# Moving the second token half's gating branch of a mixer behind the first row fetches, and the first fetched rows into attention buffers

## The reference, cut to what matters

```python
def mix_branches(q, k_all, v_all, z, gate_logits, ...):
    o = diff_attention(q, k_all, v_all, lam)
    o = rmsnorm(o, subln_g) * (1.0 - lam_init)
    y_attn = o.reshape(B, L, ATTN_OUT) @ w_branch_attn
    y_sgu = spatial_gating(gelu(z), sgu_ln_g, sgu_ln_b, sgu_w, sgu_b) @ w_branch_sgu
    g_attn, g_sgu = jnp.split(jax.nn.sigmoid(gate_logits), 2, axis=-1)
    return (g_attn * y_attn + g_sgu * y_sgu) @ w_out

def spatial_gating(z, ln_g, ln_b, w_s, b_s):
    u, v = jnp.split(z, 2, axis=-1)
    v = layernorm(v, ln_g, ln_b)
    ...
    mixed = jnp.einsum('gpq,bnqgc->bnpgc', w_s, vb) + ...
    return u * mixed.reshape(B, L, SGU_W)

def peer(h, w_query, sub_keys, u_tab, v_tab):
    q = rmsnorm((xt @ w_query).reshape(T, PEER_HEADS, 2, PEER_PK_DIM))
    s = jnp.einsum('thpd,pnd->thpn', q, sub_keys)
    # two top-16 lists a head, their 256 sums, top 16 of them: eidx, gate
    ...
    act = gelu(jnp.einsum('td,thkd->thk', xb, u_tab[ib])) * gb
    return jnp.einsum('thk,thkd->td', act, v_tab[ib])
```

## Time and profile before

| | before |
|---|---|
| median of 3 runs | 2083.95 us (2083.92 to 2088.63) |
| the profiled execution | 2088.11 us |
| its span | 2086.3 us |
| busy PE / DVE / ACT / POOL | 71% / 37% / 21% / 15% of the span |
| read from HBM | 796.98 MB, 383 GB/s on average |
| first row fetch | at 1402.00 us of the span |

### The profile page before, as it was taken

The page is one execution under the profiler, slowest core; times in us unless marked ns, Lnnn a source line. Parts: engine busy times, 40 slices in busy tenths (PEclk is TensorE's granted clock), DMA queues, the critical chain, the costliest instruction groups (busy, mean ns, idle before and its releaser), DMA issues.

```text
span 2086.3 us, 27127 instructions
## 1 busy us (share of the span) xinstructions
PE 1476.3 (71%) x11468; PEld 647.3 (31%) x11468; DVE 782.1 (37%) x1941; ACT 430.1 (21%) x1013; POOL 304.8 (15%) x290
## 2 busy tenths in 40 slices
PE   9999566877565555689899999986767744444444
PEld 7654122422111112234334445563235410000001
DVE  5832010000000000000122265547767677867764
ACT  1331100000000000011000145643245622221212
POOL 0010000000000000000000000004344444544441
PEclk9999788888878887799999999997788855555556
DMA  9798999999999999999998754469999999999997
GB/s 406 287 404 369 388 428 428 426 429 427 428 427 429 427 428 426 423 406 419 404 414 347 296 187 146 164 261 390 415 422 420 420 420 421 421 421 420 421 421 304
DMA packets 78057, 800.00 MB, mean 383 GB/s; under 512 B 9232, under 2 KB 9360, under 8 KB 10736
## 3 DMA queue, kind: packets, MB, share of 16 engines
q1 hardware_dynamic: 40304, 529.61, 60.9%
q0 software_dynamic: 37632, 268.65, 31.1%
HBM read 796.98 MB, written 1.05 MB: 383 GB/s over the span
## 4 chain that ended last, share of the span: by engine, by line
PE 42%; DMA 41%; DVE 9%; ACT 3%; issue 2%; POOL 2%; SPq 0%; DVEq 0%; ACTq 0%; POOLq 0%
DMA AR<-in_peer_uv,AR 14%; DMA AR<-in_w_gate 10%; DMA AR<-in_w_up 10%; PE PS L811 6%; PE PS L745 6%; DMA AR<-in_w_down 5%; PE PS L443 4%; PE PS L776 4%; DVE AR L1695 3%; PE PS L454 3%; PE PS L891 2%; POOL AR L2128 2%; PE PS L1027 2%; PE PS L984 2%; PE PS L707 1%
## 5 line engine op out<-in xcount | busy, mean ns | idle before, releaser
L745 PE MATMUL PS<-AR 128*32 128x512 f32 x2048 | 316.0, 751 | 200.4 <-DMA AR<-in_w_up 110.8
L1027 PE MATMUL PS<-AR 32*32 32x512 f32 x4032 | 225.5, 931 | 289.8 <-ACT AR L2063 289.7
L2128 POOL DMA_INDIRECT AR<-in_peer_uv,AR x256 | 288.8, 1128 | 967.4 <-DVE AR L1686 665.3
L1695 DVE CUSTOM_DVE_ANT_0 AR<-AR 128x1024 f32<-128x1024 f32 x256 | 309.3, 1222 | 161.7 <-DMA AR<-in_peer_uv,AR 161.3
L1323 DVE TENSOR_TENSOR AR<-AR,PS 128x512 f32<-128x512 f32 x16 | 11.0, 688 | 571.9 <-PE PS L745 571.9
L745 PEld LDWEIGHTS PS<-AR 128*32 128x32 f32 x2048 | 63.6, 124 | 422.7 <-DMA AR<-in_w_up 173.2
L776 PE MATMUL PS<-AR 128*32 128x256 f32 x2048 | 148.1, 439 | 53.5 <-DMA AR<-in_w_down 53.5
L1027 PEld LDWEIGHTS PS<-AR 32*32 32x32 f32 x4032 | 37.4, 125 | 432.6 <-ACT AR L2063 426.9
L811 PE MATMUL PS<-AR 128*128 128x512 f32 x336 | 154.2, 602 | 0.0
L776 PEld LDWEIGHTS PS<-AR 128*32 128x32 f32 x2048 | 68.8, 123 | 139.4 <-DMA AR<-in_w_down 70.0
L443 PE MATMUL PS<-AR 128*128 128x512 f32 x224 | 102.1, 610 | 1.9 <-DVE AR L1093 1.9
(11 more groups left out here) (320 smaller groups left out, 1592.3 us busy)
## 6 DMA issues: line engine op xcount, KB each, us to landing
AR<-in_w_up SPq DMA_DIRECT2D x64, 2048.0 KB, 17.4
AR<-in_w_down SPq DMA_DIRECT2D x64, 2048.0 KB, 14.5
AR<-in_w_gate SPq DMA_DIRECT2D x63, 2048.0 KB, 20.9
AR<-in_w_in SPq DMA_DIRECT2D x33, 1024.0 KB, 7.4
AR<-in_w_ada SPq DMA_DIRECT2D x12, 2048.0 KB, 13.2
AR<-in_w_out SPq DMA_DIRECT2D x6, 2048.0 KB, 8.9
AR<-in_w_in SPq DMA_DIRECT2D x5, 2048.0 KB, 14.0
AR<-in_peer_w_query SPq DMA_DIRECT2D x5, 2048.0 KB, 11.5
```

The lines of the kernel that those rows point to most:

```text
L745: x = pe.matmul(PS[32 * q:32 * q + 32, bk, :], XS[e][:, j, :], src[:, q * 512:(q + 1) * 512], start=(j == 0), stop=(j == 7), skip_group_ch ...
L1027: x = pe.matmul(PS[c:c + 32, ACC[a][g], :], DI[t, p, r, :], AR[t, off + 1024 + m * 512:off + 1536 + m * 512], start=(h == 0 and p == 0), s ...
L1695: v.tensor_tensor_reduce(rows, rows, HB[:, a, :], 1.0, 0.0, MULT, ADD, DOT[:, ix, k:k + 1]).then_inc(*w.hit("dot", ix, k))
L2128: pool.indirect_dma_start(out=AR[:, off:off + 2048], out_offset=None, in_=D["peer_uv_2"], in_offset=bass.IndirectOffsetOnAxis(ap=EI[:, ix, ...
```

## The change

Four things change together.

1. In the list of stages, `rest.z2.1 rest.z0.1 bend.z2.1 bend.z0.1 zn1.1 zn2.1 zn3.1` leave the attention part and stand between `rt5.0 qse.1.0` and `row.0.0`. `zmix.1`, `zturn.1 bend.gs.1 bs.0.1`, `bs.1.1` and `bend.ga.1` go into the row loop, at rows 2, 4, 6 and 7. From `ba.1.1` on, what `late` inserts comes 6 rows later.
2. The first five rows go to attention buffers, which are free after `av 15`; rows 5 and 6 go to the slot of the first `wq`. Two of the five are given up after row 11 (they become the buffer of w_op for half 1), one before the second half's queries.
3. SP loads z2 and z0 of half 1 into the halves of one slot, at `take.0`. w_bs 1 of half 1 takes that slot after z0 has been used. w_ba 0, w_ba 1 and w_op 0 of half 1 no longer go out at `av 15`: w_ba 0 waits for `bs.0.1`, w_ba 1 for `ba.0.1`, w_op 0 for `v.0.5` (rows 10 and 11), and so on.
4. Two small buffers move (`G2`, `SG2`), with the waits that belong to them.

```diff
-                    "rest.gs.0 bend.ga.0 bend.gs.0", "rope.q.0.1 rope.q.1.1 bs.0.0", "bs.1.0", "rest.z2.1", "rest.z0.1"]
+                    "rest.gs.0 bend.ga.0 bend.gs.0", "rope.q.0.1 rope.q.1.1 bs.0.0", "bs.1.0", "", ""]
...
-            do("bend.z2.1 bend.z0.1")
-            steps(pairs[3], [("ba", 1, 0), ("bae", 1, 0), ("zn1", 1)], pairs[4], [("yt", 0), ("yte", 0), ("zn2", 1), ("zn3", 1)])
-            steps(pairs[5], [("op", 0, 0), ("ope", 0, 0)], pairs[6], [("op", 1, 0), ("ope", 1, 0), ("zmix", 1)], pairs[7])
+            steps(pairs[3], [("ba", 1, 0), ("bae", 1, 0)], pairs[4], [("yt", 0), ("yte", 0)])
+            steps(pairs[5], [("op", 0, 0), ("ope", 0, 0)], pairs[6], [("op", 1, 0), ("ope", 1, 0)], pairs[7])
             do("rest.gs.1")
-            steps([("up1", 0), ("up2", 0)], [("zturn", 1)], pairs[8], [("fn1", 0), ("fn2", 0)], pairs[9], [("ft", 0), ("fte", 0)], pairs[10])
+            steps([("up1", 0), ("up2", 0)], pairs[8], [("fn1", 0), ("fn2", 0)], pairs[9], [("ft", 0), ("fte", 0)], pairs[10])
...
-            do("bend.gs.1 bend.ga.1 bs.0.1 bs.1.1")
+            do("rest.z2.1 rest.z0.1 bend.z2.1 bend.z0.1 zn1.1 zn2.1 zn3.1")
...
-            late = {12: [("hn1", 1)], 14: [("hn2", 1), ("ht", 1)], 18: [("hte", 1)], 22: [("ba", 0, 1)], 25: [("bae", 0, 1)],
-                    26: [("ba", 1, 1)], 29: [("bae", 1, 1)], 30: [("yt", 1)], ...
+            late = {2: [("zmix", 1)], 4: [("zturn", 1), ("bend", "gs", 1), ("bs", 0, 1)], 6: [("bs", 1, 1)], 7: [("bend", "ga", 1)], 12: [("hn1", 1)], ...
+                    32: [("ba", 1, 1)], 35: [("bae", 1, 1)], 36: [("yt", 1)], ...
...
-        RING = [3, 4, 5, 2]
+        RING = [5, 2, 3, 4]
...
-            for i, event in ((2, ("wq", 0, 0)), (0, ("w_bs", 0, 1)), (1, ("w_bs", 1, 1))):
-                free.update({k: ("used", *event) for k in halves[i]})
+            free.update({k: ("mm", "av", 15) for k in (W0 + 2048, o + 2048, o, o + 16384, o + 18432)})
+            free.update({k: ("used", "wq", 0, 0) for k in halves[2]})
...
                 elif stage == "take" and x[0] == 0:
-                    for n in range(2):
-                        square(("w_bs", n, 1), "w_branch_sgu_2", n)
-                    assert turn[0] % 4 == 2
+                    assert turn[0] % 4 == 0
+                    user[S50] = user[S51] = user[5]
+                    for slot, m in ((S50, "z2"), (S51, "z0")):
+                        load(slot, ("w_in2", m, 1), D["w_in_2"][PAIRS.index(m), 3].rearrange("p (n j c) -> p n j c", n=2, j=2), 2, 2, 512)
+                    user[5] = user[S51]
+                    turn[0] += 1
+                    square(("w_bs", 0, 1), "w_branch_sgu_2", 0)
                     for n in range(2):
                         square(("wq", n, 0), "peer_w_query_2", n)
-                    w.wait_ge("mm", "av", 15)
-                    for slot, key, name, n in ((NS, "w_ba", "w_branch_attn_2", 0), (NS + 4, "w_ba", "w_branch_attn_2", 1),
-                                               (NS + 5, "w_op", "w_out_2", 0)):
+                    square(("w_bs", 1, 1), "w_branch_sgu_2", 1)
+                    for slot, key, name, n in ((RING[1], "w_ba", "w_branch_attn_2", 0), (NS + 5, "w_op", "w_out_2", 0),
+                                               (RING[1], "w_ba", "w_branch_attn_2", 1)):
+                        if key == "w_op":
+                            for k in (o + 16384, o + 18432):
+                                w.wait_ge(*GIVEN[k])
                         load(slot, (key, n, 1), weight(name, n), 8, 512)
```

29 lines of the change are left out of this document (17 added, 12 removed), and 6 rows, old and new, of the table late.

## The result

The changed kernel takes 2135.85 us (median of 4 runs, 2132.22 to 2137.52) where the kernel before takes 2083.93 beside it: a ratio of 1.024 [1.022, 1.026], 52 us more. The forecast was 29 us more. The direction was right, the size was not, and the time lies outside the range.

The account below looks back on a forecast made before the run. The row loop was taken as bound by bytes at 421 GB/s. An earlier first row (-11.7), more bytes behind it (+20.0) and more lost time (+20.8) made +29 us on 2084: 2113 us, range 2095 to 2129.

Parts of the forecast that it names:

- Term 1: Attention chain: steps taken off it let the first row fetch start 11.7 us earlier, bounds 8 to 15.
- T0: Start of row 0, the first row fetch: 1402.00 us before the change, forecast at 1390.3.
- Term 2: Row loop: four more weight loads, 8.4 MB, move behind the first row fetch and cost 20.0 us at 421 GB/s.
- Term 3: First rows up to v.0.3: ends at T0 + 66, DMA engines stand 23.7 us against 2.9, +20.8 us.
- Later losses I leave as they are: Row loop behind v.0.3: time lost there, 4.3 us between 1435 and 1510, was taken as unchanged.
- The rival of a second starvation: Row loop at op.1.1: PE waits for the late w_op 1 load; if uncovered, 10 us more, 2123; 5 in 100.
- The fed loop: First rows: DMA engines stay fed, so term 3 is 0 or -2.9 us, time 2089 to 2092; 12 in 100.
- the faster one: Attention shrinks by 20 us and DMA engines lose nothing: -7 us, 2077; 7 in 100.
- the start that does not move: Another attention wait replaces the filler, first fetch stays at 1402: +41 us, 2125; 6 in 100.
- The late loads: Sign in the profile: four weight loads more behind the first row fetch, about 287 MB from there to the end.
- the idle times of DVE before L1516: Sign in the profile: DVE idles twice before reading bs, released by PE, 5 us and more each.

Follow-up runs that it names:

- b_order: Kernel before, with zn1.1 moved behind yte.0 and rest.gs.1 moved into a place where PE waits: 2081.1 us, ratio 0.9981.
- a_drop_one: Changed kernel without the load of w_ba 1 of half 1, its products reading w_ba 0, no wait added: 2128.98 us, ratio 1.0213.
- b_late_loads: Kernel before, with w_ba 0, w_ba 1 and w_op 0 of half 1 waiting for the row loop's second v instead of av 15: 2094.58 us, ratio 1.006.
- a_drop_early: Changed kernel without the loads of w_bs 1 and w_ba 0, their products reading w_bs 0: 2132.59 us, ratio 1.0244.
- a_spread: Changed kernel with op.1.1 at row 50 instead of 44 and what follows up to 4 rows later: 2130.84 us, ratio 1.0224.
- a_swap: Changed kernel with the loads of wq 3 and wq 0 exchanged between their two slots: 2130.33 us, ratio 1.0212.
- a_eight_late: Changed kernel with one more row buffer, the eighth, from row 36 on: 2129.2 us, ratio 1.021.
- a_swap_spread: Changed kernel with wq 3 and wq 0 exchanged between their slots and op.1.1 at row 50: 2125.44 us, ratio 1.0205.
- a_best2: Changed kernel with DVE reading bs behind rows 7 and 10, wq 3 and wq 0 exchanged, op.1.1 at row 50, extra row buffer from the start: 2109.77 us, ratio 1.0115.
- a_best: Changed kernel with z chain behind the first rows, wq 3 and wq 0 exchanged, op.1.1 at row 50, extra row buffer from the start: 2116.48 us, ratio 1.0166.
- a_z_loop: Changed kernel with the z chain behind the first rows and both bs steps two rows later: 2130.99 us, ratio 1.0226.

## Why the size was wrong, point by point

- **Term 1, T0 earlier.** Forecast 11.7, measured 11.3 as T0 - M. One trace is good to some 3 us here: the fifteen kernels with the changed attention have 195.7 to 200.9, mean 197.9, and the three with that of before 209.3 to 210.9, mean 210.0, which makes 12.1. So the sum holds. Its parts were not measured one by one, and that it came out within 0.4 us is in part luck. b_order has 6.3 us by its trace where 5.4 were expected. The 5.6 us by which T0 came earlier besides belong to the execution.
- **Term 2, bytes.** Forecast 8.4 MB and 20.0 us, measured 8.35 MB and 19.8. Where the loop is fed, a load costs its bytes (a_drop_one) or nearly (b_late_loads). Where it is not, it costs nothing (a_drop_early). The sum stays right, since term 3 took the time up to v.0.3 and subtracted all bytes in it.
- **Term 3, up to v.0.3.** Forecast T0 + 66 and 23.7 us standing, measured T0 + 72.7 and 72.7 x (1 - 245/421) = 30.4; the right mechanism, mis-sized by 6.7 us. Row 0 reached DVE at T0 + 21.2, not 19.5: the z2 products took 7.8 us (1386.64 to 1394.44) at a granted clock of 0.59, where 4.0 and 2 for the clock stood in the sum. (The terms of the forecast from DVE's sum to row 0 add up to 6.9, not to its 7.2.) The other 5.0 us lie behind row 0. 2.6 of them are the two `bs`, 9.39 + 7.13 us on PE instead of 13.9, since the first half of one ran at half the clock (below). The mixing took 2.98 instead of 1.95; the rest I have not assigned. Beside before, over the first 75 us, the loss is +25.8 where 20.8 stood in the sum.
- **"Later losses I leave as they are."** This is the step that failed. The term was put at what it had been before, without a look at what the change puts there. 13.5 us at rows 40 to 48 and 6.7 us at rows 64 to 70 were lost, 20.2, where before the same stretches lost 0.4. Three things were in the diff and not in the sum: the queries stayed while the `op` steps moved onto them (a_spread: 8.2 us off the second loss, 2.6 of them back in the third), the slot of wq 3 (a_swap: 5.5), and the missing eighth buffer (a_eight_late: 6.6). Alone they are worth 5.6, 5.5 and 6.6 us in these stretches, 17.7, and they overlap: the first two together gave 8.0 (a_swap_spread). With all three, 8.6 us are still lost there in a_best2 and 7.2 in a_best, so part of this loss has no cause shown. The rival of a second starvation had the place and one cause (PE waits 2.46 us for w_out), but it was given 5 in 100 and 10 us, and its cover was said to be eight rows, where the list of buffers has seven.
- **The other rivals.** The fed loop, the faster one and the start that does not move are all out. The late loads and the idle times of DVE before L1516 (12.57 and 7.97, "5 us and more each") came as written.

The sum, made again with what was measured: -11.3 + 19.8 + 25.8 + 19.8 (second and third loss beyond before's) = +54. The medians have +52, the two traces +49 (+55 without their 5.6 us of earlier start).

Open stays what holds the 18.0 us that a_best2 still loses in the first 75 (before: 6.4), and its 8.6 us in the second and third loss; of the first, the z chain ahead of row 0 is a part (a_z_loop: 4.9 us), and this edit was not run together with the late reading of `bs`.

## What to carry to other kernels

Where a loop is bound by transfers and fed through a few buffers, write its end as start + bytes / rate + time lost, and read the lost time stretch by stretch, for every place in which the change puts work, not only the first. At each such place compare the engine's work between two releases of a buffer with the transfers in flight (buffers x time of one), and count the buffers anew through the whole loop, since a change that borrows memory early may have one less later. A reading of PSUM that stands early in an engine's queue holds up all behind it while PE multiplies (12.57 and 7.97 us of DVE here): let PE multiply early and the reader come late.

## What the runs showed of the hardware

The two levels of TensorE's clock, in stretches of the changed kernel (busy time and instructions, granted clock, DMA share, rate):

```profile
core 0: us, PE busy (x), PEclk, DMA share, GB/s
...
1417.90:1419.80 1.90, 1.90 (x32) 0.50 0.83 349
1422.60:1427.00 4.40, 4.40 (x6) 0.50 0.95 374
1427.00:1431.90 4.90, 4.90 (x13) 0.98 0.15 62
1438.40:1439.40 1.00, 1.00 (x33) 1.00 0.12 49
```

The granted clock is 0.50 (1.2 GHz) in the `v` at 1417.87 behind an idle time of 3.35 us and in the first half of `bs.0.1` behind it, and 0.98 to 1.00 (2.4 GHz) in the second half and in the `v` at 1438.31. The same 32 products take 2.02 us at the one and 1.15 at the other. The kernel before has both as well, with a granted clock of 0.50 in the first of these `v` and 1.00 in the second:

```profile
1419.27 2.02 PE L1027 MATMUL PS<-AR 32*32 32x512 f32 x32 [1.84 <-ACT AR L2063]
...
1426.50 1.15 PE L1027 MATMUL PS<-AR 32*32 32x512 f32 x32 [0.86 <-ACT AR L2063]
```

In this chain of waits the same `bs` takes 9.39 us instead of 7.13. The length of the wait alone does not tell: the `v` at 1438.31 had waited 2.78 us and ran at 1.00, and the one at 1419.27 in the kernel before ran at 0.50 behind a wait of 1.84.

The plateau, 421 GB/s, stood at 420 or 421 over 300 us in 18 of the 19 kernels; at this rate a 2.1-MB load is 5.0 us. The prediction set it against the 358 GB/s of the Trainium skill, DMA: Bandwidth & Descriptors, Specifications. Another page of the Trainium skill, HBM Reference, Specifications (TRN2), has that figure as a core's share when both cores of a pair stream, and about 425 GB/s for a core alone, with which this trace agrees (421).

The start of the second block, by contrast, varied by 9 us between executions of unchanged code, more than the smallest gains sought here.
